# A chunked linear-attention scan on Trainium2: the old state joins the new outer products by a VectorE add in SBUF, in place of an identity matmul into their PSUM bank

## What is computed

```python
def step(state, inp):                      # state: heads x 64 x 64
    r_t, w_t, k_t, v_t, a_t, b_t = inp
    sa = jnp.einsum('bhij,bhj->bhi', state, a_t)
    state = (state * w_t[:, :, None, :] + sa[..., None] * b_t[:, :, None, :]
             + v_t[..., None] * k_t[:, :, None, :])
    return state, jnp.einsum('bhij,bhj->bhi', state, r_t)

s0 = jnp.zeros((b, RWKV_HEADS, RWKV_HEAD, RWKV_HEAD), f32)
_, y = lax.scan(step, s0, xs)
```

## Time and profile before

| what | value |
|---|---|
| median of 3 runs | 1941.69 us |
| the three runs | 1941.41, 1941.69, 1946.04 us |
| the profiled execution, its own time | 1939.81 us |
| span of that execution | 1938.0 us |
| mean granted TensorE clock | 0.961 of full |
| PE busy | 1813.1 us (94%) |
| DVE busy | 589.1 us (30%) |
| ACT busy | 362.4 us (19%) |
| POOL busy | 213.7 us (11%) |

### The profile page before, as it was taken

One profiled execution on the slowest core, in us unless ns is written; L12 is line 12 of the kernel. 1 busy time (PEld: TensorE's weight loads), 2 busy tenths in 40 slices (PEclk: granted clock), 3 DMA queues, 4 the chain that ended last, 5 costly groups with the idle time before them and its releaser, 6 DMA issues.

```text
span 1938.0 us, 25887 instructions
## 1 busy us (share of the span) xinstructions
PE 1813.1 (94%) x11066; PEld 956.5 (49%) x11066; DVE 589.1 (30%) x1265; ACT 362.4 (19%) x841; POOL 213.7 (11%) x263
## 2 busy tenths in 40 slices
PE   6979989989799999999969998999979999999993
PEld 3334347755544454444444576555554444454441
DVE  5353794452221111111040434564122111111113
ACT  2442114311100000000030113665110000000001
POOL 1044000000000000000020001454000000000002
PEclk9989999999799999999969999999979999999997
DMA  5121643060899999999969202010379999999994
GB/s 206 49 82 39 269 133 57 3 268 11 347 418 431 426 429 432 430 427 428 417 240 143 60 22 109 13 33 2 130 290 408 427 431 429 428 429 431 429 406 153
DMA packets 60786, 499.73 MB, mean 258 GB/s; under 512 B 28063, under 2 KB 28447, under 8 KB 42239
## 3 DMA queue, kind: packets, MB, share of 16 engines
q1 hardware_dynamic: 53247, 481.26, 62.1%
q0 software_dynamic: 7424, 16.80, 2.4%
HBM read 465.23 MB, written 41.18 MB: 261 GB/s over the span
## 4 chain that ended last, share of the span: by engine, by line
PE 85%; DVE 8%; issue 3%; DMA 2%; POOL 1%; ACT 1%; SPq 0%; POOLq 0%; DVEq 0%
PE bank L1390 71%; PE bank L1442 5%; PE bank L1975 3%; PE bank L1989 2%; DVE spare L1001 2%; DVE arena L1002 1%; PE bank L1775 1%; DVE arena L1253 1%; DMA arena<-y_rows,ints 1%; DMA arena<-gram_dram 1%; PE bank L1398 1%; POOL arena L491 1%; POOL arena L489 1%; DVE arena L1015 0%; PE bank L1550 0%
## 5 line engine op out<-in xcount | busy, mean ns | idle before, releaser
L1390 PE MATMUL bank<-arena 128*64 128x512 f32 (+10 forms) x5202 | 1260.5, 540 | 24.8 <-DVE arena L966 9.1
L1390 PEld LDWEIGHTS bank<-arena 128*64 128x64 f32 (+5 forms) x5202 | 485.7, 156 | 676.8 <-issue 653.6
L1390 PEld LDWEIGHTS bank<-const,arena 128*128 128x128 f32 x2048 | 237.9, 195 | 51.2 <-issue 48.7
L1390 PE MATMUL bank<-const,arena 128*128 128x128 f32 x2048 | 249.8, 281 | 2.2 <-DVE const L1132 2.2
L511 POOL DMA_INDIRECT y_rows<-arena,ints x64 | 63.0, 985 | 1124.1 <-ACT arena L747 909.5
L1207 DVE TENSOR_TENSOR arena<-arena,bank 128x256 f32<-128x256 f32 x64 | 27.0, 421 | 426.6 <-ACT arena L741 426.6
L747 ACT ACTIVATE arena<-bank 128x512 f32<-128x512 f32 x64 | 38.3, 598 | 424.2 <-PE bank L1390 424.2
L741 ACT ACTIVATE arena<-bank 128x256 f32<-128x256 f32 x64 | 24.6, 385 | 468.2 <-PE bank L1390 468.2
L1139 DVE TENSOR_TENSOR arena<-bank,vec 128x512 f32<-128x512 f32 x64 | 44.3, 692 | 192.3 <-PE bank L1390 192.3
L557 POOL TENSOR_SCALAR arena<-arena,small 128x128 f32<-128x128 f32 (+3 forms) x128 | 76.6, 609 | 150.4 <-DVE small L1367 150.4
L1216 DVE COPY arena<-bank 128x256 f32<-128x256 f32 x64 | 27.2, 424 | 184.3 <-PE bank L1775 184.3
(11 more groups left out here) (239 smaller groups left out, 972.8 us busy)
## 6 DMA issues: line engine op xcount, KB each, us to landing
arena<-m_w SPq DMA_DIRECT2D x64, 4096.0 KB, 18.8
arena<-m_w SPq DMA_DIRECT2D x64, 2048.0 KB, 16.9
y_rows<-state SPq DMA_DIRECT2D x1, 8192.0 KB, 22.6
arena<-kv_w SPq DMA_DIRECT2D x1, 6144.0 KB, 18.5
rev_bias<-arena SPq DMA_DIRECT2D x1, 5120.0 KB, 68.9
arena<-a_wk SPq DMA_DIRECT2D x2, 2048.0 KB, 14.6
arena<-a_wr SPq DMA_DIRECT2D x2, 2048.0 KB, 7.9
arena<-a_wv SPq DMA_DIRECT2D x2, 2048.0 KB, 8.1
```

Source lines behind the costliest of these rows:

```text
L1390: return nc.tensor.matmul(dst, lhsT, rhs, start=start, stop=stop)
```

## The change

In the scan, PE's identity product is gone, and the first outer product of each half now starts bank 2 afresh in every chunk, where it did so only in chunk 0. VectorE makes the new state in two stages: first it adds the bank to the old state in SBUF, one instruction for each `par`, each signalling a new semaphore `s_sum`; then it multiplies the state in place by the decay, one instruction for each `par`, each waiting for its own add. The signal `s_dve` follows the second multiplication, as it followed it before.

```diff
@@ -1043,9 +1043,14 @@
                     for par in range(2):
                         rows = slice(64 * par, 64 * par + 64)
-                        last = nc.vector.tensor_tensor(state[rows, :, 64 * par:64 * par + 64],
-                                                       bank[2][rows, :].rearrange("p (m n) -> p m n", m=NP),
-                                                       spread(chunk_decay[rows, :, c + 1], 2, 64), ALU.mult)
+                        own = state[rows, :, 64 * par:64 * par + 64]
+                        nc.vector.tensor_tensor(own, bank[2][rows, :].rearrange("p (m n) -> p m n", m=NP), own,
+                                                ALU.add).then_inc(sem("s_sum"), 1)
+                    for par in range(2):
+                        rows = slice(64 * par, 64 * par + 64)
+                        own = state[rows, :, 64 * par:64 * par + 64]
+                        dve.wait_ge(sem("s_sum"), 2 * c + par + 1)
+                        last = nc.vector.tensor_tensor(own, own, spread(chunk_decay[rows, :, c + 1], 2, 64), ALU.mult)
                     last.then_inc(sem("s_dve"), 1)
                     gram_out(c + 1, 1)
                     merge_second(c + 1)
@@ -1618,9 +1623,6 @@
                     pe.wait_ge(sem("y_act"), c)
                     for m in range(NP):
                         acc(bank[3][:, C * m:C * m + C], state[:, m, :], r_of(m)[:, c, :], m == 0)
-                    if c + 1 < NC:
-                        for par in range(2):
-                            acc(bank[2][:, :].rearrange("p (m n) -> p m n", m=NP), ident, state[:, :, 64 * par:64 * par + 64], par == 0)
                     pe.wait_ge(sem("m2_dve"), c + 1)
                     square_sums(c - 1)
                 if c + 1 < NC:
@@ -1656,7 +1658,7 @@
                     for m in range(NP):
                         for par in range(2):
                             last = acc(bank[2][64 * par:64 * par + 64, C * m:C * m + C], bkt[:, c % 2, m, 64 * par:64 * par + 64],
-                                       uv[:, c % 4, m // 4, 2 * (m % 4) + par, :], c == 0 and m == 0)
+                                       uv[:, c % 4, m // 4, 2 * (m % 4) + par, :], m == 0)
                     last.then_inc(sem("pe_s"), 1)
```

## The result

The changed kernel is slower. Its median is 1955.68 us over 5 runs (1953.34 to 1961.12), beside 1944.92 us for the kernel before over 5 runs (1941.41 to 1946.04): a ratio of 1.0065, 95% interval 1.0045 to 1.0085, some 11 to 13 us. The forecast was 1936.5 us, 0.27% faster, and the range ended at 1941.0. The profiled execution took 1955.06 us, with a span of 1953.2.

The account below looks back on a forecast made before the run. The prediction took TensorE to bound the scan, waiting each chunk for VectorE's second mask. Removing the identity product gave -10.6 us, later masks +5.5, together -5.2 unrounded: 1941.69 to 1936.5 us, range 1932.5 to 1941.0.

Parts of the forecast that it names:

- What bounds the scan, and what is waited for: In the scan: TensorE bounds; it waits for VectorE's second mask, 0.78 us later, so its pause grows 0.77 to 1.55 us.
- The term removed, -10.6 us: PE in chunks 1 to 6: dropping the identity product saves 1.77 us a chunk, 10.6 us in all.
- The term added, 5.5 us: VectorE in chunks 0 to 6: extra state instructions delay the second mask 0.78 us each, 5.5 us in all.
- The durations: VectorE's four state instructions: 0.70 us between starts, 2.79 us in all per chunk.
- the slow read: Rival: in-place state multiplications take 1.07 us, time 1942.0, or 1947.5 with slow adds; chance 0.09 shared with a hidden product.
- the cheaper SBUF source: State multiplications: by a skill table each 65 ns shorter from SBUF, 0.9 us over the scan; left out of the sum.
- The joins: Between VectorE's state instructions and to the mask: 0.70 us each without overlap; rival 0.60, 1933.8 to 1935.1 us, chance 0.14.
- the rule on held instructions: VectorE: an instruction starting in another group of 32 partitions than its predecessor waits for it, giving 0.70 instead of 0.60 us.
- The sum, -5.2 us: Whole kernel: -10.6 + 5.5, by unrounded terms -5.2 us, giving 1936.5 us; chance 0.72.
- the clock falls: Rival: PE's pause of 1.55 us per chunk in the scan halves its clock; 1957.5 us, chance 0.05.
- Its price: Clock rival in the scan: 3 us lost in each of seven chunks, 21 us in all, result +16.
- The scatter: Whole kernel: some 2 us either way, from three runs spanning 4.6 us and the half-clock stretch behind the scan.

Follow-up runs that it names:

- mask_first: Changed kernel with the second mask moved ahead of the two state multiplications, so PE's pause stays 0.77 us; 1934.45 us, ratio 0.9962 to the kernel before.
- before_dummy_fill: Kernel before plus two unused VectorE multiplications ahead of the second mask and two filler matmuls in PE's pause; 1950.74 us, ratio 1.0032.
- after_fill: Changed kernel plus two filler matmuls of 128x256 on PE in the pause before from_values; 1941.68 us, ratio 0.9987 to the kernel before.
- before_dummy: Kernel before, identity product kept, plus two unused VectorE multiplications ahead of the second mask, lengthening PE's pause; 1961.70 us, ratio 1.0079.
- before_dummy_2: Second profile of the kernel before with two unused VectorE multiplications added ahead of the second mask; 1953.26 us.
- after_fill1: Changed kernel plus one filler matmul of 128x256 on PE in the pause before from_values; 1940.21 us, ratio 0.9974 to the kernel before.
- mask_first_warm: Changed kernel with second mask ahead of the multiplications, plus filler matmuls in five PE waits ahead of and behind the scan; 1928.47 us, ratio 0.9907.
- before_warm: Kernel before plus filler matmuls in five PE waits ahead of and behind the scan, nothing changed inside it; 1941.00 us, ratio 0.9981.

## Why the prediction was wrong

- **What bounds the scan, and what is waited for**: right. The pause grew from 0.77 to 1.61 us (1.55 forecast), and the second mask followed the fourth state instruction with no idle time. The period at full clock was 14.64 us (14.6 forecast).
- **The term removed, -10.6 us**: right; 10.63 in mask_first, which has that term alone.
- **The term added, 5.5 us**: right in kind, slightly low; 5.73 in before_dummy_fill, and 10.63 - 4.65 = 6.0 in the changed kernel's order (after_fill).
- **The durations**: right. The multiplication out of SBUF took 687 ns, the add 688, so neither the slow read (1074 ns) nor the cheaper SBUF source came. The joins cost 0.70 to 0.73 us each, and with this the trace agrees with the rule on held instructions that I quoted from the Trainium skill ("VectorE: DVE Perf Modes", section "Two Vector instructions with no wait between them"). The rows, over the chunk: two adds 325.60 to 327.04, two multiplications to 328.46.
- **The sum, -5.2 us**: after_fill's scan gives -4.65 at full clock. The changed kernel itself came out 11 to 15 us slower, because the sum had no term for the clock.
- **The step that failed** is in the rivals, "the clock falls", which had 0.05. The mechanism was stated rightly: a pause of 1.55 us in every chunk brings the clock down. What put it aside was "PE stays busy for about nine tenths of the time, and 13.0 us lie between two pauses", and that was no evidence: the chunks of before held pauses of 0.77 us only, so they could not say what one of 1.55 does. The runs showed that it does bring the clock down: two to four falls of 3.4 or 10.2 us in the scan, in five of five profiles with pauses of 1.57 to 1.61 us. Of the falls of before I had weighed only the one behind the scan. Another, from 285.4 to 292.4 us, reaches into what is called the scan ahead of the prediction (from 287 us), beside a pause of 5.30 us that ends at 287.19. And further ahead the profile of before has a longer pause with a fall right behind it, though also one of 1.25 us at 201.89 and one of 1.39 at 296.30 with none (two views below this list). The example in the section of the Trainium skill that I quoted there ("TensorE: Matmul & The Clock Gate", section "HAM oscillation — how this bites in real kernels") has waits of 3 to 5 us, not of 1.6, so "exactly such a cycle" said too much. The trace agrees with its direction, though not with a fall at each wait: two to four falls came on seven pauses.
- **Its price** was mis-built as well: I had 3 us for a fall and seven falls, +16 in all. The scan lost 10.3 us by two falls in two profiles and 15.1 by four in the third. I had no term for the tail, where a fall of 24 to 27 us in all three profiles of the changed kernel takes the place of one of 6.8: +6.2 to +6.5 us. It begins at the last of the long pauses or within 2 us of it; but before_dummy had such a pause there and no long fall, so the pause alone doesn't decide it.
- **Summed from the ledger**: -4.65, +10.3 to +15.1, +6.4, which is +12 to +17, and about -2.5 in the rest of the program; the medians differ by 11 and 15 us. The -2.5 goes with the long tail: the rest took 1488.7 to 1489.1 us in the four profiles that have one (before_dummy_2 among them), and 1490.3 to 1494.8 in the nine others.
- **The scatter**: I allowed 2 us either way, from three runs. 17 to 29 runs of the same kernel span 13 to 14 us. One fall ahead of the scan, at a place where PE waits 1.25 us, makes some 5 us of that; the rest is open.

The pause in the profile of before that ends at 182.75 us, and the stretch behind it:

```profile
182.75 1.66 PE L1390 MATMUL bank<-arena 128*128 128x512 f32 x2 [1.33 <-issue]
```

```profile
183.00:186.60 3.60, 3.60 (x5) 0.61 (x5) 0.55 (x2) 0.95 (x1) 3.60 (x4) 0.53 0.33 71
```

## What to carry to other kernels

Work taken from the bounding engine is worth its full time only if its pauses do not grow: before forecasting a gain, list that engine's pauses per period with their lengths, and treat a longer pause than any the trace shows at full clock as a risk of its own, not as a small one. Put what the bounding engine waits for ahead of what it needs later: here the reordering of two VectorE steps made a loss of 0.65% into a gain of 0.4%. And where TensorE must wait, filler matmuls into a dead bank can be tried; here they cost nothing, as they ended before the wait did (the distance between chunks stayed 14.65 us).

## What was unexpected of the hardware

- A scan in which PE was busy 14.39 of 16 us lost its clock by pauses of 1.6 us; no fall came behind pauses of 0.51 to 1.09 us in the same place, in any of eight profiles (0.51 in before_dummy_fill, 0.55 in after_fill, 0.98 and the last one 1.09 in after_fill1, 0.77 in two of before and one each of mask_first, mask_first_warm and before_warm).
- A fall is no fixed length. Behind the scan it lasted 6.8 us in two profiles of before, 24 to 27 in three of the changed kernel; ahead of the scan 30.7 us, while PE was busy 32.00 of 32 us. There PE ran, without a pause, products with 128 rows of weights and, in turn with them, 16 with 32.
- Falls repeat by position: two profiles of the changed kernel that shared the fall at 200 us had the later ones up to the tail within 1 us of each other; the third had neither that one nor, in the scan, those positions.
